# Two-block transformer kernel, one core: centring products of the heads' norm issued together, three panels of the output projection begun on the memory tiles

## The reference, cut to what matters

```python
mean = jnp.mean(y, axis=-1, keepdims=True)
var = jnp.mean(jnp.square(y - mean), axis=-1, keepdims=True)
y = ((y - mean) * lax.rsqrt(var + LNX_EPS)).reshape(B, S, BR_W) * lnx_w + lnx_b
return y + bonus.reshape(B, S, BR_W)
...
y = jnp.concatenate([(y_br * jax.nn.silu(gate.astype(jnp.float32))).astype(x.dtype),
                     y_mem * jax.nn.silu(g_mem)], axis=-1) @ w_out[l]
x = x + rms_norm(y, post_norm[l])
```

## Time and profile before

| What | Value |
|---|---|
| median of 3 executions | 1290.06 us |
| lowest and highest | 1288.85 and 1290.41 us |
| the profiled execution's own time | 1289.03 us |
| its span, first to last instruction | 1287.2 us |
| what lies around the span | 1.83 us |
| mean granted TensorE clock over the span | 0.974 of full speed |
| TensorE busy (matmuls) | 1202.5 us, 93% |
| VectorE busy | 849.0 us, 66% |
| ScalarE busy | 626.9 us, 49% |
| GpSimd busy | 187.4 us, 15% |
| share of TensorE in the chain that ended last | 76% |

### The profile page before, as it was taken

One profiled execution on the slowest core, in us unless ns is written; L12 is line 12 of the kernel. 1 busy time (PEld: TensorE's weight loads), 2 busy tenths in 40 slices (PEclk: granted clock), 3 DMA queues, 4 the chain that ended last, 5 costly groups with the idle time before them and its releaser, 6 DMA issues.

```text
span 1287.2 us, 23943 instructions
## 1 busy us (share of the span) xinstructions
PE 1202.5 (93%) x9724; PEld 1155.8 (90%) x9724; DVE 849.0 (66%) x1460; ACT 626.9 (49%) x1075; POOL 187.4 (15%) x186
## 2 busy tenths in 40 slices
PE   5989699898996899999999999989999999999997
PEld 5978587698996899999989999879999999999997
DVE  4769845776675686655497745669556668867643
ACT  5765342663556554444243445453445545645541
POOL 1127040200002021110022000005100001122101
PEclk8999789998998999999999999999999999999999
DMA  6443220244452565556335542335454345755560
GB/s 225 134 129 116 83 67 34 97 137 144 132 160 83 177 213 180 169 157 182 114 121 192 165 131 88 110 101 197 162 180 149 130 155 173 253 189 183 156 203 33
DMA packets 53677, 186.83 MB, mean 145 GB/s; under 512 B 6720, under 2 KB 8896, under 8 KB 53184
## 3 DMA queue, kind: packets, MB, share of 16 engines
q1 hardware_dynamic: 53008, 183.07, 44.0%
q10 hardware_dynamic: 560, 2.24, 0.5%
HBM read 184.24 MB, written 1.05 MB: 144 GB/s over the span
## 4 chain that ended last, share of the span: by engine, by line
PE 76%; DVE 13%; ACT 7%; issue 3%; DMA 1%; POOL 0%; DVEq 0%; SPq 0%; ACTq 0%; POOLq 0%
PE bank L2560 21%; PE bank L2563 20%; PE bank L2561 20%; DVE wl L1998 4%; ACT wh L1624 2%; PE bank L2577 2%; PE bank L2594 2%; PE bank L2581 1%; PE bank L2578 1%; PE bank L2545 1%; PE bank L2603 1%; DVE zl L2105 1%; DVE sqr L2109 1%; DVE tmp L2473 1%; DVE tmp L2471 1%
## 5 line engine op out<-in xcount | busy, mean ns | idle before, releaser
L1998 DVE TENSOR_TENSOR wl<-raw,wh 128x1024 fp32r<-128x1024 f32 (+1 forms) x343 | 423.0, 1242 | 205.7 <-ACT wh L1624 202.1
L2560 PE MATMUL bank<-xh,wh 128*128 128x256 f32 (+1 forms) x1880 | 545.3, 290 | 1.4 <-ACT wh L1624 1.1
L2563 PE MATMUL bank<-xh,wl 128*128 128x256 f32 (+1 forms) x1880 | 537.3, 286 | 7.6 <-DVE wl L1998 7.4
L2561 PE MATMUL bank<-xl,wh 128*128 128x256 f32 (+1 forms) x1880 | 537.4, 286 | 0.0
L1624 ACT ACTIVATE wh<-raw 128x1024 fp32r<-128x1024 f32 (+1 forms) x343 | 355.2, 1044 | 271.5 <-PE bank L2563 257.8
L2563 PEld LDWEIGHTS bank<-xh,wl 128*128 128x128 f32 x1880 | 359.2, 191 | 10.0 <-DVE wl L1998 9.8
L2560 PEld LDWEIGHTS bank<-xh,wh 128*128 128x128 f32 x1880 | 357.5, 190 | 6.8 <-issue 3.3
L2561 PEld LDWEIGHTS bank<-xl,wh 128*128 128x128 f32 x1880 | 358.4, 191 | 0.5
L2560 PE MATMUL bank<-hh,wh 128*128 128x272 f32 (+1 forms) x352 | 100.3, 285 | 0.0
L2561 PE MATMUL bank<-hl,wh 128*128 128x272 f32 (+1 forms) x352 | 100.2, 285 | 0.0
L2563 PE MATMUL bank<-hh,wl 128*128 128x272 f32 (+1 forms) x352 | 100.2, 285 | 0.0
(11 more groups left out here) (377 smaller groups left out, 1732.4 us busy)
## 6 DMA issues: line engine op xcount, KB each, us to landing
raw<-w_ffn_gate SPq DMA_DIRECT2D x44, 512.0 KB, 3.6
raw<-w_ffn_up SPq DMA_DIRECT2D x44, 512.0 KB, 3.7
raw<-w_a_w_in SPq DMA_DIRECT2D x29, 512.0 KB, 3.5
raw<-w_ffn_down SPq DMA_DIRECT2D x32, 448.0 KB, 3.4
raw<-w_w_out SPq DMA_DIRECT2D x16, 512.0 KB, 3.5
raw<-w_b_w_in SPq DMA_DIRECT2D x16, 512.0 KB, 4.5
raw<-w_ffn_down SPq DMA_DIRECT2D x16, 512.0 KB, 3.6
raw<-w_ret SPq DMA_DIRECT2D x16, 512.0 KB, 3.7
```

What stands on the lines that cost most here:

```text
L1998: v.tensor_tensor(lo[:, c], raws[n % N_RAW][:, c], hi[:, c].bitcast(F32), ALU.subtract).then_inc(*w_lo.up(n))
L2560: pe.matmul(ps, hi[:, c], x_hi(k), start=(k == 0), stop=False)
L2561: pe.matmul(ps, hi[:, c], x_lo(k), start=False, stop=False)
L2563: last = pe.matmul(ps, lo[:, c], x_hi(k), start=False, stop=(k == kt - 1))
```

## The change

`OUT_BEGUN = (3, 2)` says how many panels `begin_out` takes in each layer: three in layer 0, two as before in layer 1. The splits of panel 2 are issued by `prefetch(3)` ahead of `step_y(1)`, no longer inside `begin_out`. `branch0(3)` stands inside `step_y(1)`, after its step i = 2. The three `norm_a` steps come first, then `norm_b(0)`, `begin_out`, `norm_b(1)`, `branch0(0)`, `norm_b(2)`, `branch0(1)` and `branch0(2)`.

```diff
@@ build: schedule
+OUT_BEGUN = (3, 2)
...
             def begin_out(layer, part):
-                return begin([(f"w_out{layer}", panel, f"y{layer}", S, out_evac(layer)) for panel in range(2)], part)
+                return begin([(f"w_out{layer}", panel, f"y{layer}", S, out_evac(layer)) for panel in range(OUT_BEGUN[layer])], part)
...
                 finish(begun)
-                for panel in range(2, KT):
+                for panel in range(OUT_BEGUN[layer], KT):
...
                     do("y", c, i, b, freed)
                     bank.give(b, (yd, (c, i)))
+                    if c and i == 2:
+                        do("branch0", 3)
...
             next(head[1], None)
+            prefetch(3)
             step_y(1)
...
-            do("branch0", 3)
-            da0 = norm_a(0)
-            begun = begin_out(0, (6, 7))
-            norm_b(0, da0)
-            da1 = norm_a(1)
-            norm_b(1, da1)
-            da2 = norm_a(2)
-            do("branch0", 0)
-            norm_b(2, da2)
-            do("branch0", 1)
+            centred = [norm_a(j) for j in range(3)]
+            for j, da in enumerate(centred):
+                norm_b(j, da)
+                if j:
+                    do("branch0", j - 1)
+                else:
+                    begun = begin_out(0, (6, 7))
             do("branch0", 2)
```

## The result

The changed kernel is slower: 1292.26 us (median of 13 executions, 1290.89 to 1293.62) against 1289.18 us (13 executions of the kernel before beside it, 1287.78 to 1290.45). The ratio is 1.0024 with an interval of 1.0015 to 1.0032, so 3.1 us (1.9 to 4.1). This ratio, here and in the experiments, need not be the quotient of the two medians (in experiment 1 it is 0.9995 where that is 0.9984); whether a kernel is faster or slower is read from the interval of the ratio. The forecast was 1289.8 us and "no difference"; the range ended at 1291.8. The profiled execution took 1291.54 us with a span of 1289.7 us.

The account below looks back on a forecast made before the run. TensorE, busy 93% of the span, was taken as the bound; -0.72 us from order plus 0.5 us of clock loss gave -0.2 us, 1289.8 against 1290.06 us, range 1288.0 to 1291.8.

Parts of the forecast that it names:

- What bounds the kernel, and the early steps: TensorE, busy 93%, gains only where it stands still: the 5.4 us before layer 0's closed projection stream; first sum at 227.50.
- The two moves: Panel 2's split and the gated memory tiles, moved among or ahead of the last heads' products, fit existing waits: cost 0.
- the step-by-step sum: Layer 0's steps from first centring to projection end, in the new order at full clock: -0.72 us.
- The stall for panel 3: In layer 0's projection, TensorE waits for panel 3's split, 242.82 to 244.83; the lead shrinks from 2.5 to 0.72 us.
- VectorE fitted its queue in behind it: VectorE's subtractions, evacuations and memory tiles behind panel 3's split end before panel 6's subtraction is needed, by 0.7 us.
- Net 0.25 to 1.5 us; I take 0.5: Clock falls in or after TensorE's new 3.3 us gap, 232.4 to 235.74; loss taken as 0.5 us.
- one low stretch as long as those of the earlier trace: After the new gap, 3 to 3.5 us of low clock as in layer 1, losing 0.8 to 1.5 us.
- the slack ahead of tiles 2 and 3: Wait for xl of group 1, 237.9 to 238.44, said to absorb up to 0.55 us of clock loss.
- the clock falls there too: Rival: at panel 3's stall, 242.8 to 244.8, another 1.5 us lost; with the first gap +2.3, 1292.3 us; chance 0.1.
- What follows the last panel hangs on that panel alone, so the 0.72 us pass on whole: Evacuation, splits and residual behind layer 0's projection depend only on the last panel, so the whole 0.72 us gain remains.
- a stage behind 260 longer by over 1 us at the same clock: Sign of a wrong prediction: any stage after 260 us changing length by over 1 us with the same clock.

Follow-up runs that it names:

- experiment 1: Changed kernel with two panels begun in layer 0 instead of three: 1287.01 us against 1289.06 for the kernel before, ratio 0.9995.
- experiment 4: Kernel before with only panel 2's split and the gated memory tiles moved ahead of the last products: 1289.42 against 1289.06 us, ratio 1.0005.
- experiment 6: Changed kernel with seven matmuls of constants in TensorE's wait ahead of tiles 0 and 1: 1288.48 us against 1288.84 for the kernel before, ratio 1.0002.
- experiment 7: Changed kernel with two begun panels and seven matmuls of constants in the wait: 1289.68 us against 1288.84 for the kernel before, ratio 1.0006.
- experiment 12: Changed kernel with two begun panels, run again unaltered: 1286.55 us against 1289.14 for the kernel before, ratio 0.9976.
- 4 added to the change: Changed kernel with four matmuls of constants (1.74 us) ahead of panel 4: 1292.10 us, ratio 1.0030 to the kernel before.
- 2 added: Changed kernel with two matmuls of constants (0.87 us) ahead of panel 4: 1292.46 us, ratio 1.0028 to the kernel before.
- 3 and 4 added to before: Kernel before with three or four matmuls of constants between the begun panels and panel 2: 1290.37 and 1291.29 us, ratios 1.0010 and 1.0013.
- experiment 3: Kernel before with only three panels begun, old order of the norm: 1291.92 against 1289.06 us, ratio 1.0030.
- experiment 2: Kernel before with only the three centrings put first: 1289.04 against 1289.06 us, ratio 1.0003.
- experiment 10: Kernel before with three matmuls of constants (1.30 us) between the begun panels and panel 2: 1290.37 against 1289.14 us, ratio 1.0010.
- experiment 11: Kernel before with four matmuls of constants (1.74 us) between the begun panels and panel 2: 1291.29 against 1289.14 us, ratio 1.0013.

## Why the prediction was wrong

**What bounds the kernel, and the early steps: right.** The first sum is 2.68 us behind the first centring (forecast 2.66), the first logarithm 3.74 (3.72), the second 6.73 (6.72), the matmuls of tiles 0 and 1 10.90 (10.90). The two moves cost nothing, and experiment 4 shows their gain alone, 0.97 us of stage. At full clock the change leaves 33.97 us of stage (experiment 6); the step-by-step sum gave 34.03.

**The stall for panel 3: right.** It was forecast as a break from 242.82 to 244.83 with two matmuls in it, 2.01 us, and measured from 243.91 (the group's last start and one distance more) to 245.83, 1.92 us, of which 0.50 and 0.76 us are rows of waiting. The 1.06 us between experiments 6 and 7 are the net price of the third panel. VectorE fitted its queue in behind it with no further wait.

**The clock: the term that was mis-sized.** The step "Net 0.25 to 1.5 us; I take 0.5" failed. It costs 2.1 us. Two things were wrong. I gave the fall one low stretch as long as those of the earlier trace rows, while the clock here stays low from inside the wait at 231.43 to 234.78 until 240.7. And I took the slack ahead of tiles 2 and 3 as a cover for it, while the slack is 0.55 us and a block of 18 at half clock overruns it by more. By the rows: 26 starts from 235.16 on, up to 240.70, at 0.213 instead of 0.119 us and 0.38 instead of 0.23 us from the first matmul to the second (experiment 6), make 2.6 us, less the 0.5 us of slack. One reading was off: in the earlier trace rows the clock falls at 292.8 us, 1.2 us after the wait of 1.03 us has ended at 291.57, and not 0.9. The rival "the clock falls there too" at panel 3 did not happen; its +2.3 us would have given 1292.3 us, almost the measured 1292.26, but by luck: the 2 us behind the stage that it lacked have another cause.

**"What follows the last panel hangs on that panel alone, so the 0.72 us pass on whole": wrong.** The dependences do hang on it alone, and the first 30 us behind the stage are alike. But the time of the rest depends on where the clock's falls meet it. The 1.3 us of the stage put layer 1 at a place where the falls cost 2.1 to 2.3 us more, in three of three traces of the changed kernel; the earlier trace rows showed the falls that this works through, and I used them as prices only. The forecast had listed a stage behind 260 longer by over 1 us at the same clock as a sign against it; here it is longer at a lower clock.

The sum by its parts, for the traced execution: -0.78 us of order at full clock, +2.1 us of clock in the stage, +2.1 us behind it, 3.4 us in all; the medians moved by 3.1 to 4.3. (The two profiled executions differ by 2.51 us only, since the stage of the changed one began 0.96 us earlier.) The executions without a trace agree: the mean granted clock of all 27 of the changed kernel is 0.969 to 0.973 but for one at 0.976, middle value 0.971, and that of the kernel before, run beside the experiments, 0.974 to 0.980. Between 0.971 and 0.976 lie some 13 us more of low clock (an estimate: twice the difference times 1290 us). That is more than the 6.8 us that the stage alone has, though the part ahead of the stage, low for 24 to 38 us in the traces, is in these means too.

**The question of what would have been better.** The third panel is the part that does not pay: it adds 1.06 us of stage at full clock with the stall for panel 3 as its rows, and it puts more matmuls behind the long wait, at half clock. Without it the version of experiments 1 and 12 is 2.1 and 2.6 us lower at the median than the kernel before, but with ratios of 0.9995 and 0.9976 only the second is clear of 1. That it is faster than the kernel before is not shown.

**What stays open.** Why the medians of the delayed kernels follow their traces in one case (4 added to the change) and not in others (2 added; 3 and 4 added to before). Each kernel has one to three traces, and the other executions give only a time and a mean clock. The rest repeats in the two traces of the kernel before and the three of the changed one, and does not in the two of the version with two panels. The time ahead of the stage, which differs by 5.5 us between traces, moves each execution too.

## What to carry to other kernels

Gathering small steps in front of a serial chain can join several short waits of TensorE into one long one, as here (3.35 us). Price the long wait with the whole work behind it at half clock, and compare with the slack there, before counting what the order wins. A group that holds every split buffer makes the panel behind it wait for its own split (here 0.50 and 0.76 us). And where waits and clock falls follow the edit, a difference of some 2 us in total is no measure of the edit itself: compare the stage in two traces, look at where in the spread of times the traced execution lies, and put a known delay into the old kernel to see what a pure shift does.

## What the runs showed of the hardware

A wait of 1.37 us between blocks left the clock full. Around one of 1.83 us (experiment 3) and around those of 3.35, 3.36 and 4.27 us (the change, experiments 1 and 2) it fell; in the earlier trace rows it also fell behind one of 1.03 us. But the length of the wait does not settle it: the clock fell in a wait of 3.34 us in experiment 10 and stayed full through the same wait, 3.35 us, in experiment 11. After a fall the clock did not come back with the next block at once: in the changed kernel 26 matmuls ran at 0.21 us each. Seven matmuls on constants (14 records, 3.0 us) in the wait kept it full. The Trainium skill (TensorE: Matmul & The Clock Gate, section HAM oscillation — how this bites in real kernels) says that a block behind a long wait for data starts at the lower clock. The change and experiments 1 and 2 agree, with the 2.1 us of experiment 6 as its price here; experiment 11 does not.

I had not expected that 1.29 us of added work could lengthen a traced execution, from the first centring on, by 3.5 us, and 1.70 us by 0.2 (experiments 10 and 11), with the instructions behind it unchanged and the granted clock of later stretches different. The medians show less of it, +1.2 and +2.2 us.
